# Prompt attention in a hybrid decoder step: visiting the query tiles of a head as 0, 7, 1, 6, 2, 5, 3, 4

## What is computed

```
for h in range(4):                      # heads
    for i in range(8):                  # query tiles of 128 tokens
        fox = softmax(q k^T + c_q - c_k, keys 0 .. 128*(i+1))  @ v
        slc = softmax(q k^T + bias,      keys 0 .. 128*(i+1))  @ v_s   # all 16 blocks are selected
        win = softmax(q k^T + bias,      keys of tiles max(0,i-4) .. i) @ v_w
        cmp = softmax(q k^T + bias,      8*i+7 compressed keys, at most 63) @ v_c
        o_fox = fox ; o_nsa = g0*cmp + g1*slc + g2*win
```

## Time and profile before

| what | us |
|---|---|
| median of 3 runs | 1297.93 (1296.79 to 1302.99) |
| the profiled execution | 1296.74 |
| its span, first to last instruction | 1294.9 |
| attention stage, scores of step 0 to the last values | about 542 to 784 |
| one interior head, first scores to first scores of the next | 57.9 |
| head 3, first scores to the end of its last iteration with scores | 51.3 |

### The profile page before, as it was taken

The page is one execution under the profiler, slowest core; times in us unless marked ns, Lnnn a source line. Parts: engine busy times, 40 slices in busy tenths (PEclk is TensorE's granted clock), DMA queues, the critical chain, the costliest instruction groups (busy, mean ns, idle before and its releaser), DMA issues.

```text
span 1294.9 us, 21298 instructions
## 1 busy us (share of the span) xinstructions
PE 1175.4 (91%) x7638; PEld 694.1 (54%) x7638; DVE 741.2 (57%) x1753; ACT 415.5 (32%) x905; POOL 172.8 (13%) x181
## 2 busy tenths in 40 slices
PE   6999999999999999879898999999838999999980
PEld 4686776766766455657566665545424333333320
DVE  6943774845734012587878783344865334444776
ACT  4332533424313011347575772232300111111331
POOL 0131041220301000300000000000000111111243
PEclk9999999999999999989999999999958999999995
DMA  9850120220201312405010005400267987676984
GB/s 285 268 146 7 35 66 8 53 42 19 83 1 51 119 26 40 129 11 161 9 44 1 18 18 176 154 33 33 71 242 271 314 309 245 242 240 249 349 314 161
DMA packets 126836, 163.19 MB, mean 126 GB/s; under 512 B 32193, under 2 KB 101105, under 8 KB 126742
## 3 DMA queue, kind: packets, MB, share of 16 engines
q1 hardware_dynamic: 111590, 108.32, 27.8%
q0 software_dynamic: 15152, 53.60, 11.4%
HBM read 224.77 MB, written 36.45 MB: 202 GB/s over the span
## 4 chain that ended last, share of the span: by engine, by line
PE 72%; DVE 16%; DMA 4%; issue 3%; ACT 3%; SPq 2%; POOL 0%; DVEq 0%; ACTq 0%; POOLq 0%
PE act L715 17%; PE vec L1310 10%; PE vec L1036 8%; PE vec L750 8%; PE act L961 4%; PE vec L949 4%; PE vec L783 2%; PE act L973 2%; DMA arena<-x_rows,arena 2%; PE vec L1323 2%; PE act L1323 2%; PE act L986 2%; PE vec L725 1%; DVE arena L2031 1%; SPq L483 1%
## 5 line engine op out<-in xcount | busy, mean ns | idle before, releaser
L715 PE MATMUL act<-arena 128*128 128x352 f32 x768 | 237.3, 464 | 1.2 <-ACT arena L1404 1.2
L715 PEld LDWEIGHTS act<-arena 128*128 128x128 f32 x768 | 143.0, 190 | 77.1 <-ACT arena L1404 1.7
L1310 PE MATMUL vec<-arena 128*64 128x512 f32 x768 | 175.8, 610 | 1.9 <-DMA arena<-in_exp_w 1.9
L1036 PE MATMUL vec<-arena 128*128 128x512 f32 x256 | 114.6, 601 | 0.8 <-DVE arena L2056 0.8
L1310 PEld LDWEIGHTS vec<-arena 128*64 128x64 f32 x768 | 54.2, 139 | 103.8 <-issue 102.1
L750 PE MATMUL vec<-arena 128*128 128x512 f32 (+1 forms) x256 | 100.3, 546 | 0.0
L1557 ACT ACTIVATE arena<-arena 128x640 f32<-128x640 f32 (+15 forms) x128 | 81.3, 639 | 8.9 <-DVE arena L2031 8.8
L2379 DVE TENSOR_SCALAR arena<-arena 128x256 f32<-128x256 f32 x24 | 7.1, 296 | 133.2 <-ACT arena L1654 133.1
L2031 DVE CUSTOM_DVE_ANT_0 arena<-vec,arena 128x128 f32<-128x128 f32 (+6 forms) x168 | 69.0, 430 | 22.4 <-PE vec L949 15.4
L1548 ACT COPY arena<-act 128x512 f32<-128x512 f32 (+11 forms) x176 | 63.2, 430 | 55.5 <-PE act L961 55.2
L961 PE MATMUL act<-arena 128*128 128x128 f32 (+4 forms) x440 | 66.7, 289 | 15.2 <-DVE arena L2047 14.6
(11 more groups left out here) (450 smaller groups left out, 1903.9 us busy)
## 6 DMA issues: line engine op xcount, KB each, us to landing
arena<-in_exp_w SPq DMA_DIRECT2D x192, 512.0 KB
arena<-in_exp_w SPq DMA_DIRECT2D x48, 1024.0 KB
y_rows<-arena POOLq DMA_DIRECT2D x24, 512.0 KB, 6.1
arena<-in_w_in SPq DMA_DIRECT2D x16, 512.0 KB, 6.8
arena<-in_x_prompt SPq DMA_DIRECT2D x8, 512.0 KB, 6.3
x_spill<-arena POOLq DMA_DIRECT2D x8, 512.0 KB, 3.4
arena<-x_spill SPq DMA_DIRECT2D x8, 512.0 KB, 5.1
arena<-in_cache_fox_kv SPq DMA_DIRECT2D x16, 256.0 KB, 3.5
```

What stands on the lines that cost most here:

```text
L715: last = mm(bk[:, 0:n], W[k % 2][:, c, m * P:(m + 1) * P], xT[:, c, a:a + n], start=c == 0, stop=c == NC - 1)
L1036: last = mm(bk[:r], src, Wo[half][:, c, :], start=c == 0, stop=c == NC - 1)
L1310: last = mm(gu_bank[p][o], xgT[p][:, c, o], Wgu[:, slot, c, :], start=c == 0, stop=c == NC - 1)
```

## The change

The tiles of every head are taken in another order. Nothing else is edited: the same 64 steps, the same instructions, the same positions for `decay_rows`, for POOL's addition and for the strips.

```
-    PAIRS = [(h, i, kinds) for h in range(H) for i in range(8) for kinds in (("fox", "slc"), ("win", "cmp"))]
+    PAIRS = [(h, i, kinds) for h in range(H) for i in (0, 7, 1, 6, 2, 5, 3, 4) for kinds in (("fox", "slc"), ("win", "cmp"))]
```

## The result

The changed kernel takes 1318.22 us (median of 4 runs, 1315.56 to 1330.09), the kernel before 1298.18 us. The ratio is 1.0165, with a 95% interval of 1.0109 to 1.0222: slower by 1.1 to 2.2%, as forecast (1319, range 1307 to 1328). The ratios and their intervals leave out one slow execution, of experiment 9 (1754.66 us at a mean granted clock of 0.647).

The account below looks back on a forecast made before the run. PE sets the pace, DVE close behind. Waits of 34.3 us against 17.0 add 17.3, the low clock 4.2: 1296.74 + 17.3 + 4.2 = 1318.2; with the run median 1.2 above the profiled execution, 1319 us, range 1307 to 1328.

Parts of the forecast that it names:

- The mechanism: Attention stage: the DVE and ACT chain grows with its own step, PE's cover with earlier steps; large tiles now follow small.
- The wait behind F7: PE waits 3.2 us: about 1.0 for W0's probabilities, then 2.2 for F7's; chain 9.06 us against 5.83 of PE work.
- the sign of being wrong: Prediction wrong if the wait before F7's 16 transposes is under 1 us, or DVE still reduces when PE reaches W1.
- The whole of a head's waits: PE's new waits: 9.0 us each in heads 1 and 2, 7.8 in head 3, 7.7 in head 0.
- Behind F6, F5 and F4: PE's waits at tiles 6, 5 and 4: about 2.1, 1.4 and 0.8 us; chains 8.7, 8.3 and 7.5.
- the terms named for the cover: Tiles 6, 5, 4: small partner's transposes, values, scores gain 0.21 each, large scores lose 0.21; cover 6.5, 6.9, 6.7 us.
- the calibration: F7's chain in the kernel before, pieced together from the profile: 9.29 us, 9.56 with a 0.27 us DVE wait, against 9.61.
- The sum of waits: PE's waits over four heads and the hand-over to the output projection: 34.3 us against 17.0, so +17.3 us.
- The clock: PE at the 1.2 GHz level behind F7 in three of four heads, 1.4 us each: +4.2 us; bounds 0 and 11.
- The heads: Expected in the changed profile: a head of about 62 us for heads 1 and 2, 57 for head 3.
- Position 8: Heads 0 to 2: W6's scaling meets POOL's addition, PE waits 2.8 to 3.2 us; 0.6 us more if they share bandwidth.
- The rival "faster": Mixing large with small tiles removes all waits but POOL's three, giving 1289 us; chance 4 in 100.

Follow-up runs that it names:

- experiment 9: On the kernel of experiment 5, DVE's add_halves placed ahead of normalise in its iteration; 1298.26 us, ratio 0.999 to the kernel before.
- Experiment 1: Kernel before with order 0, 7, 1, 2, 3, 4, 5, 6: one large tile behind a small one, the rest growing; 1314.01 us, ratio 1.012.
- experiment 2: Kernel before with the smooth order 0, 2, 4, 6, 7, 5, 3, 1, neighbours at most two tiles apart; 1293.39 us, ratio 0.9971.
- experiment 5: Changed kernel with PE's transposes three iterations behind the scores instead of two, values four; 1289.63 us, ratio 0.9935 to the kernel before.
- experiment 4: Changed kernel with POOL's addition held back until F2's probabilities are scaled; 1311.73 us, ratio 1.012 to the kernel before.
- Experiment 3: Changed kernel with unused spare matmuls filling PE's waits before W0's, F7's and W6's transposes; 1306.30 us, ratio 1.007 to the kernel before.
- experiments 5 and 6: Transposes three iterations behind the scores, values four: 5 in the changed order, 1289.63 us; 6 in the kernel before's growing order, 1300.96 us, ratio 1.0001.
- experiment 7: Kernel before, growing order, with POOL's addition held back until F4's probabilities are scaled; 1288.74 us, ratio 0.9899.

## Why the prediction was right

- **The mechanism** held: the chain behind a step is as long as that step, its cover as long as the steps before. Experiment 1 has the same two gaps from one jump alone, experiment 2 has no loss without a jump, and experiment 5 gives the loss back when only the cover is lengthened. Experiment 1 also shows the limit of the sum of waits as a forecast: there it explains 3.2 of the 21.8 us.
- **The wait behind F7** was put at 1.0 + 2.2 us and is 0.96 + 1.98 in heads 1 to 3. In head 0 it is 0.42 us before F7's transposes, under the 1 us that the prediction named as the sign of being wrong; there PE's own work beside the chain ran at the low clock (0.55 from 562.0 to 567.9) and so filled more of it. In experiment 4 the same wait of head 0 is 1.41 us. The whole of a head's waits was put at 9.0 and is 9.1 in heads 1 and 2; in head 3, 7.7 against 7.8. Behind F6, F5 and F4 PE waited 1.9 (head 3), 1.2 and 0.8 us (heads 0 to 2), where 2.1, 1.4 and 0.8 were forecast. These had luck in them: the terms named for the cover (three gains of 0.21, one loss of 0.21) make 6.25, 6.67 and 7.09 and not 6.5, 6.9 and 6.7. Two smaller slips changed nothing: the calibration leaves 0.05 us (9.61 less 9.56) and not 0.07, and the forget rows stand in the sum with 3.2 us and in the text with 3.1.
- **The sum of waits**, +17.3, is 3.2 too high: +14.1. Head 0 waits 6.2 us and not 7.7; F7's work fills 1.3 us of the waits of the key compression, which I left out; and the baseline was some 0.6 us larger than the 17.0 us, which leave out the 0.54 us before F1's transposes.
- **The clock**, +4.2, was too low: 9 to 11.4 us in the profiled execution, about 6 in the median run. I let three of four heads fall to the low level behind F7; in the profile the low clock was there in all four. The two misses cancel to about 1 us, so the closeness of 1319 to 1318.2 is in part luck. Experiment 3 shows that the clock's part is real, and larger than the change's own share.
- **The heads** took 64.0, 65.6 and 58.9 us, not 62 and 57. Those figures held the new waits but not the clock, an omission of mine.
- **Position 8**: wait 3.19, 3.20 and 3.58 us, forecast 2.8 to 3.2. W6's 640 columns took 0.08 us more than W3's 512, not 0.6. DVE's scaling ends 0.51 us after POOL, and takes 0.71 alone: it is held for nearly all of POOL's addition and then does its work; the two do not share. That agrees with the Trainium skill, SBUF — State Buffer, section "SBUF: two separate sides".
- **The rival "faster"** failed here, as the chain was longer than the cover, but its idea is sound: with one more iteration of cover the mixed order beats growing order by 8 to 11 us (experiments 5 and 6). The prediction did not see that the two belong together.

## What to carry to other kernels

In a software pipeline like this one, a step is covered by the work of the steps before it, not by its own. Before reordering, write down for the largest step the chain through the other engines and the bound engine's work inside the same distance; if the chain is longer, either deepen the pipeline first or keep the sizes changing in small steps, down as well as up. Price the low clock apart from the waits: in experiment 1 it was nearly the whole loss. Then look for the collision of two engines in the trace: here one added wait on POOL's queue was worth 1.0%, where the order of the tiles cost 1.65%.

## What was new about the hardware

- POOL's 2.34 us addition of 1024 columns held DVE's SBUF-to-SBUF scaling (0.71 us alone, 2.62 beside it), but left DVE's reductions from PSUM with their SBUF bias at 0.69 us each (experiment 7). What may run beside POOL depends on the DVE instruction.
- PE fell to the 1.2 GHz level after two gaps of 0.96 and 1.98 us with 1.5 us of work between, and stayed at 2.4 GHz behind single gaps of 0.72 us. Spare matmuls in the gaps before W0, F7 and W6 were worth 11.9 us of 1318.
- The same kernel's executions differed in their mean granted clock: 0.949 in that of 1330.1 us, 0.956 in that of 1315.6 us.
